# Loading c, half of the modulation and the constants in a new order at launch, in a two-layer hybrid diffusion block

## The reference, cut to what matters

```
mod_l = (jax.nn.silu(c) @ w_ada[l] + b_ada[l]).reshape(b_, 1, N_MOD, D_MODEL)
mod_c = (jax.nn.silu(c_ctx) @ w_ada[l] + b_ada[l]).reshape(N_MOD, D_MODEL)
def _pre(x, nw, shift, scale):
    return rmsnorm(x, nw) * (1 + scale) + shift
xl = _ffn_sublayer(xl, mod_l, 0, nw[0], nw[1], w_ff_in[l, 0], w_ff_out[l, 0])
```

## Time and profile before

| what | value |
|---|---|
| median of 3 runs | 2924.2 us (2924.07 to 2924.86) |
| span of the profiled execution, first to last instruction | 2921.0 us |
| TensorE busy | 2750.3 us, 94% of the span |
| VectorE busy | 1458.4 us, 50% |
| ScalarE busy | 869.2 us, 30% |
| transfers | 315.81 MB, mean 108 GB/s |
| granted TensorE clock, mean | 0.974 |

### The profile page before, as it was taken

The page is one execution under the profiler, slowest core; times in us unless marked ns, Lnnn a source line. Parts: engine busy times, 40 slices in busy tenths (PEclk is TensorE's granted clock), DMA queues, the critical chain, the costliest instruction groups (busy, mean ns, idle before and its releaser), DMA issues.

```text
span 2921.0 us, 35967 instructions
## 1 busy us (share of the span) xinstructions
PE 2750.3 (94%) x14448; PEld 2459.3 (84%) x14448; DVE 1458.4 (50%) x1967; ACT 869.2 (30%) x1152; POOL 80.2 (3%) x40
## 2 busy tenths in 40 slices
PE   5999998998988989999999999999998988799998
PEld 2999997887966789999988899999887756688887
DVE  2555556655444665555465555554464555532233
ACT  3211112443422351111235511112353423522232
POOL 0000000100000110000001000000000000100001
PEclk9999999999989999999999999999999999799999
DMA  5333333332200233333343333333332301322231
GB/s 213 123 115 122 130 133 136 140 129 77 94 0 1 73 116 115 115 122 124 121 171 125 130 115 120 123 131 116 129 115 91 108 1 44 115 101 100 87 129 72
DMA packets 100973, 315.81 MB, mean 108 GB/s; under 512 B 6928, under 2 KB 23312, under 8 KB 87312
## 3 DMA queue, kind: packets, MB, share of 16 engines
q1 hardware_dynamic: 93744, 297.20, 29.3%
q10 hardware_dynamic: 7136, 17.30, 1.7%
HBM read 312.38 MB, written 2.10 MB: 108 GB/s over the span
## 4 chain that ended last, share of the span: by engine, by line
PE 87%; DVE 7%; ACT 2%; issue 2%; DMA 1%; POOL 0%; SPq 0%; POOLq 0%; DVEq 0%; ACTq 0%
PE ps L1529 46%; PE ps L1543 23%; PE ps L795 5%; PE ps L902 2%; PE ps L1572 2%; DVE w_lo L1266 2%; PE ps L1601 1%; PE ps L1611 1%; PE ps L885 1%; ACT w_hi L1059 1%; PE ps L876 1%; DVE acc L1292 1%; PE ps L938 1%; PE ps L1585 1%; PE ps L895 1%
## 5 line engine op out<-in xcount | busy, mean ns | idle before, releaser
L1529 PE MATMUL ps<-xn_hi,w_hi 128*128 128x384 f32 (+2 forms) x2528 | 725.2, 342 | 21.8 <-DVE arena L1351 16.9
L1529 PE MATMUL ps<-xn_lo,w_hi 128*128 128x384 f32 (+2 forms) x2528 | 721.6, 340 | 0.0
L1529 PE MATMUL ps<-xn_hi,w_lo 128*128 128x384 f32 (+2 forms) x2528 | 721.4, 340 | 0.0
L1266 DVE TENSOR_TENSOR w_lo<-raw,w_hi 128x2048 fp32r<-128x2048 f32 x211 | 499.6, 2368 | 375.7 <-ACT w_hi L1059 375.4
L1529 PEld LDWEIGHTS ps<-xn_hi,w_hi 128*128 128x128 f32 x2528 | 464.3, 189 | 33.9 <-issue 17.3
L1059 ACT ACTIVATE w_hi<-raw 128x2048 fp32r<-128x2048 f32 x211 | 400.5, 1898 | 283.7 <-PE ps L1543 225.8
L1529 PEld LDWEIGHTS ps<-xn_lo,w_hi 128*128 128x128 f32 x2528 | 465.5, 189 | 11.3
L1529 PEld LDWEIGHTS ps<-xn_hi,w_lo 128*128 128x128 f32 x2528 | 465.4, 189 | 11.0
L1162 ACT ACTIVATE arena<-ps 128x384 f32 (+3 forms) x158 | 72.8, 496 | 1102.8 <-PE ps L1529 1102.7
L1292 DVE SCALAR_TENSOR_TENSOR acc<-raw_ada,silu_c,acc 128x512 f32<-128x512 f32 x512 | 345.5, 746 | 4.5 <-DVE acc L1280 3.2
L1543 PE MATMUL ps<-w_hi,hj_hi 128*128 128x512 f32 x952 | 301.2, 398 | 17.7 <-DVE w_lo L1266 8.2
(11 more groups left out here) (183 smaller groups left out, 2288.5 us busy)
## 6 DMA issues: line engine op xcount, KB each, us to landing
raw<-w_ff_in SPq DMA_DIRECT2D x104, 1024.0 KB, 5.3
raw<-w_ff_out SPq DMA_DIRECT2D x77, 1024.0 KB, 4.8
raw_ada<-w_ada SPq DMA_DIRECT2D x128, 512.0 KB, 3.7
raw<-w_out SPq DMA_DIRECT2D x16, 1024.0 KB, 4.8
raw<-w_in SPq DMA_DIRECT2D x12, 1024.0 KB, 5.2
arena<-w_ada SPq DMA_DIRECT2D x4, 2048.0 KB, 17.5
gate_row<-norm_w ACTq DMA_DIRECT2D x12, 512.0 KB, 4.2
arena<-dft_l_in ACTq DMA_DIRECT2D x2, 2048.0 KB, 7.9
```

The costliest lines, as they stand in the source:

```text
L1266: nc.vector.tensor_tensor(w_lo[par][:, 0:width], raw[par][:, 0:width], w_hi[par][:, 0:width].bitcast(F32), ALU.subtract).then_inc(S["w_lo" ...
L1529: ins = mm(ps[:, 4 * b + part + c, col:col + wd], w[:, k, c, :], xx[:, k, t0:t0 + wd], start=(k == 0 and i == 0), stop=(k == KC - 1 and i ...
```

## The change

`cvec` gets a semaphore of its own, `c_in`, and silu waits for it alone. After c, SyncE issues three of the small loads (b_col, nw_col, tri), then halves 0 and 1, then the other four small loads (convw, convb, hn_w, gate_b), half 2, slot 0 of w_ff_in, and half 3. ScalarE issues the six loads of x after silu, once half 0 has landed. VectorE waits for the seven loads that still count on `consts`.

```diff
--- before.py
+++ after.py
@@ -307,7 +307,7 @@
 
         S = {}
         for name in (
-            "consts pool_consts dve_consts x_in "
+            "c_in consts pool_consts dve_consts x_in "
             "w_raw0 w_raw1 w_hi w_lo w_used "
             "ada_raw0 ada_raw1 ada_used fin_mm fin_read row_mm row_read silu_c "
             "silu h_done hj_hi hj_lo "
@@ -980,14 +980,21 @@
                 src = w_ada[l].rearrange("(u c p) n -> u p c n", c=2, p=P)[u, :, :, bass.ds(col, HB)]
                 sp.dma_start(raw_ada[u % 2][:], src).then_inc(S[f"ada_raw{u % 2}"], 16)
 
-            for dst, src in ((cvec[:], cvec_in), (b_col[:], b_col_in), (nw_col[:], nw_col_in), (convw[:], convw_in),
-                             (convb[:], convb_in), (hn_w[:], hn_w_in), (tri, tri_in), (gate_b[:], gate_b_in)):
-                sp.dma_start(dst, src).then_inc(S["consts"], 16)
-            for i in range(4):
-                if i == 3:
-                    load(0, 0, w_ff_in[0, 0, 0])
+            def first_half(i):
+
                 src = w_ada[0].rearrange("(k p) n -> p k n", p=P)[:, :, i * HB:(i + 1) * HB]
                 sp.dma_start(ada0(i), src).then_inc(S["ada_first"][i], 16)
+
+            sp.dma_start(cvec[:], cvec_in).then_inc(S["c_in"], 16)
+            for dst, src in ((b_col[:], b_col_in), (nw_col[:], nw_col_in), (tri, tri_in)):
+                sp.dma_start(dst, src).then_inc(S["consts"], 16)
+            first_half(0)
+            first_half(1)
+            for dst, src in ((convw[:], convw_in), (convb[:], convb_in), (hn_w[:], hn_w_in), (gate_b[:], gate_b_in)):
+                sp.dma_start(dst, src).then_inc(S["consts"], 16)
+            first_half(2)
+            load(0, 0, w_ff_in[0, 0, 0])
+            first_half(3)
 
             for sub in SUBS:
                 l, j, n0 = sub["l"], sub["j"], sub["slot"]
@@ -1141,10 +1148,11 @@
                 for c in range(2):
                     hj(sub, 0, c, 2 * nb + c, nb % 2 * 2 + c)
 
+            act.wait_ge(S["c_in"], 16)
+            nc.scalar.activation(silu_c[:], cvec[:], ACT.Silu).then_inc(S["silu_c"], 1)
+            act.wait_ge(S["ada_first"][0], 16)
             for t in range(NT):
                 act.dma_start(x[:, t, :], x_in[t]).then_inc(S["x_in"], 16)
-            act.wait_ge(S["consts"], 16 * 8)
-            nc.scalar.activation(silu_c[:], cvec[:], ACT.Silu).then_inc(S["silu_c"], 1)
             act.wait_ge(S["x_in"], 16 * NT)
             act.wait_ge(S["pool_consts"], 2)
             for t in range(NT):
@@ -1377,7 +1385,7 @@
                     hj(sub, 0, c, sub["hj"] + c, 2 * nb + c, nb % 2 * 2 + c)
 
 
-            dve.wait_ge(S["consts"], 16 * 8)
+            dve.wait_ge(S["consts"], 16 * 7)
             dve.wait_ge(S["pool_consts"], 2)
             nc.vector.tensor_copy(ident_bf[:], ident[:])
             nc.vector.tensor_scalar(mask[:], tri, -1.0, -NEG, ALU.add, ALU.mult).then_inc(S["dve_consts"], 1)
```

## The result

The changed kernel took 2929.03 us (median of 20 runs, 2926.5 to 2932.6), the kernel before 2923.63 (20 runs, 2920.3 to 2926.3). The ratio is 1.0021, 95% interval 1.0014 to 1.0027, so the change costs 0.21%, 4 to 8 us; the medians differ by 5.4 us. Measured once more on another chip beside the last experiments it was 1.0023 (1.0011 to 1.0035). The forecast was 2930.7 against 2924.2, a ratio of 1.0022.

The account below looks back on a forecast made before the run. One long TensorE program fills nearly all of the span; the change touches only the launch ahead of it. The copy, the later of two branches, moves from 27.37 to 33.85: 2924.2 + 6.5 = 2930.7 us, range 2927.0 to 2933.8.

Parts of the forecast that it names:

- The copy as the later of two branches: At launch, VectorE's copy of half 0's rows waits for P or X, whichever is later: 33.85 against 27.37, 6.5 us later.
- P: Launch chain: small loads landed, then ident_bf and mask, then TensorE's sixteen matmuls; puts the copy at 33.85 us.
- X: Launch chain: x landed, then ScalarE's and VectorE's statistics up to the last reciprocal, 9.76 us; puts the copy at 33.55.
- the sum of the packets: Launch transfers: two halves 10.8 us and x 8.1 us end at 22.7; x landed at 23.75, gate_b at 24.15.
- From copy to end, one to one: After the copy no wait hangs on the launch's loads, so its delay delays the end one to one: 6.5 us.
- The sharing of the queues: At launch both queues share the engines packet by packet: equal counts between 12 and 20 us, about 63 each in a microsecond.
- Rival A: At launch, an engine takes a whole load's share of a ring before turning to the other queue: +6.0, 2930.2; chance 0.10.
- Rival B: At launch, the queues share by bytes throughout, so x lands at 28.95, copy at 38.7: +11.4, 2935.6; chance 0.05.
- Rival C: At launch, x is served first and the small loads don't wait for half 1: +3.2, 2927.4; chance 0.11.
- D: At launch, the sooner half pays: TensorE starts at 10.5, copy at 19.7: -7.7, 2916.5; chance 0.01.
- E: Over the long rest, TensorE's clock gives it back by sparing 25 us of half-rate time: -6.0, 2918.2; chance 0.04.
- F: After the launch, the rest takes the delay up, no change that counts: 2924 to 2926; chance 0.03.

Follow-up runs that it names:

- e3: Changed kernel with the four late small loads on a semaphore of their own, which VectorE waits for after ident_bf and mask; 2933.7 us, ratio 1.0036.
- e5: Changed kernel with VectorE's six reciprocals moved behind the second half's copy, the wait for seven small loads kept; 2933.1 us, ratio 1.0014.
- e4: e3 with VectorE's six reciprocals and the wait for the late small loads moved behind the second half's copy; 2915.6 us, ratio 0.9973.
- e8: Kernel before with only VectorE's reciprocals moved behind the second copy; 2927.5 us, ratio 0.9999.
- e1: Changed kernel with its order of SyncE's loads kept, but x issued at once as in the kernel before; 2929.4 us, ratio 1.0023.
- e9: e3 with one more wait: TensorE holds its first matmul back until x has landed; 2933.9 us, ratio 1.0013.
- e2: Changed kernel with all seven small loads ahead of half 0, x still issued only when half 0 has landed; 2936.1 us, ratio 1.0042.
- e6: Changed kernel with ScalarE issuing x when half 1 has landed, not half 0; 2948.9 us, ratio 1.0067.
- e12: The same program as e4, run again on the third chip; 2920.8 us, ratio 0.9973.

## Why the prediction was right, point by point

| step | forecast | changed kernel |
|---|---|---|
| half 0 issued, landed | 2.6, 10.4 | 2.61, 10.74 |
| x issued | 10.45 | 10.76 |
| gate_b landed | 24.15 | 23.6 |
| first matmul | 24.7 | 24.12 |
| x landed | 23.75 | 24.6 |
| copy of half 0's rows | 33.85 | 34.30 |
| first turn | 59.8 | 60.17 |
| loss | 6.5 | 6.7 by the spans, 5.4 by the medians, 4 to 8 by the ratio |

The measured 2929.03 lies inside the range for 8 in 10, and 1 us below the 2930.0 with which the prediction's own account began; part of that is the kernel before, which came out at 2923.63 and not 2924.2.

**The copy as the later of two branches** was right and is shown from three sides: e3 and e5 open one each and win nothing or 1 us, e4 opens both and wins 15.2 us at the copy, e8 shows that the second branch did not count before. Which branch came last was called wrongly: I had P by 0.3, it was X by 0.3. That cost nothing, for the reason given there: both tails are alike, and the sum of the packets does not ask for the order. That branch P ended at 34.0, close to its 33.85, was luck: gate_b landed 0.55 us sooner than forecast, and the sixteen matmuls took 9.84 us where the sum had 9.15. Over all fourteen profiles these first sixteen took 8.3 to 9.8 us, a scatter for which the sum had no term.

**From copy to end, one to one.** From the copy to the first product it is 40.0 us in the kernel before (27.37 to 67.40), the changed one (34.30 to 74.31), e1 (33.17 to 73.21), e5, e8 and e9. It is 42.9 in e2, 43.0 in e3 and 41.7 in e6, the three in which TensorE idled long between first and second half. So the step holds for this change, and has a condition which I had not stated: TensorE must not have gone idle ahead of the copy. In the changed kernel the late small loads kept it from that by accident. e9 against e3 shows that these 3 us are the lower clock's.

**The sharing of the queues.** Equal packet counts were forecast for 12 to 20 us and found from 15 on: 66 and 67 while half 1 still ran, 98 and 99 beside the small loads. Rival A wanted two to one while half 1 ran and falls; with it falls, for these two queues as the profile counts packets, the reading of the Trainium skill ("DMA: Bandwidth & Descriptors", Queues, rings and completion order) by which an engine would drain a packet of many such rows before it switches. Equal groups of many rows would give equal counts too, but tenths of a microsecond rule them out: from 14.5 us on, x's rows came as 9 and 7, then 2, 13 and 1, so sixteen, one for each engine, every quarter of a microsecond, with half 1's between them. Rival B (shares by bytes) falls by the same rows. But x's first packets came later than I had them, at 14.5 and not at 11.65: q1 had all the traffic till then. Half 1 was the faster for it, and the small loads stood nearly all beside x. They were through before x was, and then rows of half 2 went in turn with x's last ones, 0.12 and 0.14 MB in 22 to 23 and 23 to 24 us. The sum had nothing of half 2 ahead of x's end. At the 387 GB/s of the prediction these rows and those of 21 to 22 (0.04 MB) are an estimated 0.8 us, about what x was late: it landed 0.85 after its forecast.

**Rival C** (small loads pass the half) is refuted by gate_b's 15.5 us from issue to landing, and **D** (the sooner half pays) by the same wait; e4 shows what D needed. **E** and **F** (the clock or the rest gives it back) have no support: mean granted clock 0.974 in both profiles, and the first product 6.9 us late against a span 6.7 longer.

**What was off.** I took the scatter of this kernel from three runs within 0.8 us. Twenty runs spread over 6 us on one chip, and 29 over almost 20 on another. A loss just above 0.2% was as near to that bound in the measurement as in the forecast: the ratio is 1.0021, and the 5.4 us between the medians are just under 0.2%. That the change slows the kernel is clear of noise; that it does so by more than 0.2% is not.

## What to carry to other kernels

A load that is brought forward pays only if nothing else that its user needs has gone behind it: write down, for the first instruction that uses it, every wait ahead of it on every engine of the chain, and look for one semaphore that counts late loads together with early ones. When two branches end together, removing either one shows nothing; remove both before a load order is called useless. And transfers on several queues share one set of engines, so put the sum of all bytes that move before the join against the time, with those of loads that nobody waits for yet but that go in turn with one that is waited for. In the changed kernel and in e2 rows of half 2 were such bytes.

## What the runs showed of the hardware that I had not expected

- Starting TensorE early can cost time. After 17 and 16 us idle between two like pieces of work its second half took 9.7 and 9.8 us (e2, e3), after 19 us 8.5 (e6), against 7.03 in every other profile; the granted clock at the end of these gaps was 0.50 of 2.4 GHz. Held back until x had landed, it lost nothing against the changed kernel (e9). A short gap is not always harmless: after 1.0 us of waiting e4's third half took 8.72 us, after 0.7 us that of e12, the same program, took 7.03. What decides between the two is not shown.
- x's first packets moved 3.7 us after their issue at 10.76, and as long after it in e2 and e6, each time while q1 kept the engines busy; the first transfers of an idle chip began 1.2 us after theirs. That the busy queue is the cause fits, but no run isolates it.
- An issue can take long: SyncE stood 9.05 us in its issue of a 36 KB load behind two of 2 MB (e1), 3.3 us in the changed kernel, against 0.43 in the kernel before, where no large load stood ahead of it in SyncE's queue. Small loads behind large ones were late by the issue as well as by the queue.
